# A hybrid encoder block: second chunk loaded with the first, later keys put back, merge's first attention rows in a buffer of their own, aligned tiles and equal score pieces

## The reference

```python
h = rmsnorm(x, g_norm_mix); proj = h @ w_in            # 1024 x 5168, split into the parts below
y_att = dsa_attention(q, k, v, q_idx, k_idx, w_idx)    # a relu indexer scores every visible key, the best 256 of a query are attended
y_mlstm = sigmoid(mo) * rmsnorm(mlstm_chunkwise(...))  # 4 heads of 128, causal convolution on q and k, scan over chunks
merged = sigmoid(ga) * (y_att @ w_proj_att) + sigmoid(gm) * (y_mlstm @ w_proj_mlstm)
x = x + merged @ w_out
return x + hierarchical_moe(rmsnorm(x), ...)           # 4 groups of 8 experts, top 1 group, top 2 experts
```

## Time and profile before

| | us |
|---|---|
| three runs | 3384.41, 3392.61, 3396.44 (median 3392.61) |
| the profiled execution | 3387.83, its span 3386.2 |
| TensorE busy in the span | 3001.3 (89%) |
| VectorE busy | 2481.9 (73%) |
| ScalarE busy | 1815.9 (54%) |
| TensorE's granted clock, mean | 0.949 of full speed |
| transfers | 545.93 MB, mean 161 GB/s |

### The profile page before, as it was taken

The page is one execution under the profiler, slowest core; times in us unless marked ns, Lnnn a source line. Parts: engine busy times, 40 slices in busy tenths (PEclk is TensorE's granted clock), DMA queues, the critical chain, the costliest instruction groups (busy, mean ns, idle before and its releaser), DMA issues. The chain is left out here.

```text
span 3386.2 us, 44801 instructions
## 1 busy us (share of the span) xinstructions
PE 3001.3 (89%) x12983; PEld 2228.0 (66%) x12984; DVE 2481.9 (73%) x3912; ACT 1815.9 (54%) x2527; POOL 462.2 (14%) x603
## 2 busy tenths in 40 slices
PE   7998899799899957899989689999399999999990
PEld 5766778578678724455545367787388888888870
DVE  6577599789899956766663354443799999999985
ACT  5322467577578433444434333332377777777770
POOL 0211110000000042211111000000111111111114
PEclk9999999899999979999999899999699999999995
DMA  3222533232212185536432375552578879667868
GB/s 125 88 74 70 145 119 116 77 125 86 75 60 72 66 178 123 117 90 118 91 68 65 106 214 171 164 173 93 198 267 307 333 278 364 226 254 257 309 249 340
DMA packets 382434, 545.93 MB, mean 161 GB/s; under 512 B 36624, under 2 KB 217536, under 8 KB 382160
## 3 DMA queue, kind: packets, MB, share of 16 engines
q1 hardware_dynamic: 351536, 434.81, 42.2%
q0 software_dynamic: 28448, 100.94, 7.9%
q10 hardware_dynamic: 2304, 8.39, 0.6%
HBM read 510.70 MB, written 138.19 MB: 192 GB/s over the span
## 5 line engine op out<-in xcount | busy, mean ns | idle before, releaser
L916 DVE TENSOR_TENSOR e_w_lo<-e_raw,e_w_hi 128x1024 fp32r<-128x1024 f32 x386 | 447.0, 1221 | 4.3 <-ACT e_w_hi L773 4.3
L1585 PE MATMUL x_ps<-h_hi,w_hi 128*128 128x512 f32 (+1 forms) x992 | 391.8, 395 | 6.0 <-PEq L90 4.5
L1585 PE MATMUL x_ps<-h_lo,w_hi 128*128 128x512 f32 (+1 forms) x992 | 390.1, 393 | 0.0
L1585 PE MATMUL x_ps<-h_hi,w_lo 128*128 128x512 f32 (+1 forms) x992 | 389.6, 393 | 0.0
L773 ACT CAST e_w_hi<-e_raw 128x1024 fp32r<-128x1024 f32 x386 | 377.5, 1055 | 5.7 <-PE e_pG L711 5.7
L2362 DVE CUSTOM_DVE_ANT_0 t_junk<-t_L,t_mask 128x512 bf16<-128x512 f32 (+3 forms) x320 | 186.0, 608 | 180.8 <-PE t_L L2142 179.5
L1772 DVE TENSOR_SCALAR_CACHE_REDUCE x_relu<-x_score,x_cand 128x1024 uint8<-128x1024 f32 (+3 forms) x217 | 315.7, 1487 | 3.6
L1687 ACT ACTIVATE x_relu<-x_score,x_cand 128x896 int8<-128x896 f32 (+3 forms) x217 | 281.5, 1298 | 61.9 <-DVE x_cand L1779 61.6
L2181 PE MATMUL t_O<-t_probT,t_v 128*65 128x512 f32 x544 | 288.8, 613 | 21.7 <-ACT t_probT L2334 18.7
L2334 ACT ACTIVATE t_probT<-t_ST 128x512 f32<-128x512 f32 x272 | 160.4, 594 | 271.2 <-PE t_ST L2173 270.7
L711 PE MATMUL e_pG<-e_w_hi,e_x_hi 128*128 128x512 f32 x768 | 246.8, 403 | 3.6 <-DVE e_x_lo L911 2.4
(11 more groups left out here) (415 smaller groups left out, 6266.7 us busy)
## 6 DMA issues: line engine op xcount, KB each, us to landing
e_raw<-in_w_exp_gate SPq DMA_DIRECT2D x392, 256.0 KB
e_raw<-in_w_exp_up SPq DMA_DIRECT2D x392, 256.0 KB
e_raw<-in_w_exp_down SPq DMA_DIRECT2D x192, 512.0 KB
projT<-x_out SPq DMA_DIRECT2D x120, 256.0 KB, 2.8
slot_out<-e_y POOLq DMA_DIRECT2D x48, 512.0 KB
w_raw<-in_w_in SPq DMA_DIRECT2D x40, 512.0 KB
o_gate<-projT SPq DMA_DIRECT2D x32, 512.0 KB
slot_out<-x_zeros SPq DMA_DIRECT2D x31, 512.0 KB
```

The source lines that it names most:

```text
L916: nc.vector.tensor_tensor(w_lo[:, u, :], raw[:, u, :], w_hi[:, u, :].bitcast(F32), ALU.subtract).then_inc(gl, 1)
L1585: last = nc.tensor.matmul(ps[0:w, u % 4, :], wt[:, m % 2, kk, 0:w], ht[:, kk, q * 512:(q + 1) * 512], start=(kk == 0 and s == 0), stop=(kk ...
```

## The change

- `pieces(n)` cuts a block of more than 1024 keys in equal pieces of whole 128-key blocks. The count of pieces stays. The planner's total changes with the count of 512-column matmuls.
- In the attention stage the queries of block 0 are issued by ScalarE and no longer first on SP. Quarters 2 and 3 of the keys are loaded at f = 28 and 60 and no longer at f = 3 and 7. Chunk 1 is loaded right behind chunk 0 at f = 23 and no longer at f = 34.
- In the merge the attention rows of group 0 have a buffer of their own, `Y0`, which lies over `XN` (`XN` is first written after them), and are issued before gate 0, weights 1 and gate 1, with no wait.
- Tiles are declared in another order, and 480 bytes are put behind the router's bias, so that the large tiles of the last three stages start at multiples of 512 bytes.

```diff
 def merge_and_output(pg, LG, BI):
...
-        SUM, YR, REC = sb("sums", [P, 32]), sb("y", [P, 4, W]), sb("inverse", [P, 4, W])
+        YR, REC = sb("y", [P, 4, W]), sb("inverse", [P, 4, W])
...
+        Y0 = XN[:, :, :].rearrange("p a (b n) -> p (a b) n", n=W)
...
-                    if x >= 4:
+                    if x >= 4 and g:
                         sp.wait_ge(yl, 8 * g + x - 3)
...
-                    sp.dma_start(YR[:, k % 4, :], src[:, k % 4, g * W:(g + 1) * W]).then_inc(y_in[k], 16)
+                    sp.dma_start((YR if g or k >= 4 else Y0)[:, k % 4, :], src[:, k % 4, g * W:(g + 1) * W]).then_inc(y_in[k], 16)
...
             proj_weights(0)
             rows(0, ORDER[:4])
             inverses(0)
+            rows(0, ORDER, 4)
             gates(0)
             proj_weights(1)
             gates(1)
-            rows(0, ORDER, 4)
...
-                    v.tensor_tensor(REC[:, k, :], REC[:, k, :], YR[:, k, :], ALU.mult).then_inc(n_ok, 1)
+                    v.tensor_tensor(REC[:, k, :], REC[:, k, :], (YR if g else Y0)[:, k, :], ALU.mult).then_inc(n_ok, 1)
...
 def pieces(n):
-    return [(a, min(width(n), a + 1024)) for a in range(0, width(n), 1024)]
+    step = P * -(-(n + 1) // -(-width(n) // 1024))
+    return [(a, min(width(n), a + step)) for a in range(0, width(n), step)]
...
 def attend_and_recur(pg):
...
-            load(0)
             load_keys(0)
             load(1)
...
-                if f in (3, 7):
-                    load_keys(2 + f // 7)
+                if f in (28, 60):
+                    load_keys(2 + f // 60)
...
                 k = chunk_at(f, -13)
-                if k:
+                if k and k > 1:
                     load_chunk(k)
                 if f == CHUNK0 - 9:
                     load_chunk(0)
+                    load_chunk(1)
...
+            for k in range(2):
+                act.dma_start(Q[k * AD:(k + 1) * AD, 0, :, :].bitcast(F32), queries(0)[0]).then_inc(q_in[0], 16)
+            act.dma_start(Q2[0:AD, 0, :, :].bitcast(F32), queries(0)[1]).then_inc(q_in[0], 16)
...
 def build(nc, ins, out):
...
+        c.enter_context(nc.sbuf_tensor("to_512_bytes", [P, 120], F32))
```

More of the change, by code:

```diff
@@ L144, in merge_and_output @@
         X, XN, XT, SQ = sb("x", [P, 2, DM]), sb("xn", [P, 2, DM]), sb("xT", [P, KT, P]), sb("sq", [P, DM], BF16)
-        G, WR = sb("gain", [P, DM]), sb("wr", [P, KT, NR])
+        Y0 = XN[:, :, :].rearrange("p a (b n) -> p (a b) n", n=W)
+        G, WR, SUM = sb("gain", [P, DM]), sb("wr", [P, KT, NR]), sb("sums", [P, 32])
         ss, rt, rs = (sb(n, [P, 2]) for n in ("ss", "rt", "rs"))
@@ L499, in route_and_experts @@
         w_hi, w_lo = sb("w_hi", [P, NU, 1024], F32R), sb("w_lo", [P, NU, 1024], F32R)
-        IX, IXF = sb("ix", [P, NBLK + 2], I32), sb("ix_f", [P, NBLK])
-        XG, ix = sb("xg", [P, 2, DM]), sb("ix_now", [P, 2], I32)
+        XG, Y, work = sb("xg", [P, 2, DM]), sb("y", [P, DM]), sb("work", [P, XBUF, DM])
+        IX, IXF, ix = sb("ix", [P, NBLK + 2], I32), sb("ix_f", [P, NBLK]), sb("ix_now", [P, 2], I32)
         x_hi, x_lo = sb("x_hi", [P, KT, P], F32R), sb("x_lo", [P, KT, P], F32R)
@@ L1865, in attend_and_recur @@
         sem = pg.semaphores(c, "t_")
+        idb, mxp = sb("ident_b", [P, P], BF16), sb("max_part", [P, 2, R4, 4])
         KS, K2 = sb("k", [P, AKV, SEQ], F32R), sb("k_shift", [P, AKV, SEQ], F32R)
-        V = sb("v", [P, NT, AKV, AD + 1])
         Q, Q2 = sb("q", [P, 4, AH, P], F32R), sb("q_shift", [P, 4, AH, P], F32R)
         MB = sb("mask", [P, 4, SEQ], BF16)
+        X, MN, WI = sb("m_X", [P, 2, 4, MH, P]), sb("m_MN", [P, 2, MH, P]), sb("m_WI", [P, 2, MH, P])
+        CY, YM, GN = sb("v_Y", [P, 3, 512]), sb("m_Y", [P, 2, MH, P]), sb("m_gain", [P, MH, MD])
+        OU, DEC = sb("out", [AD + 1, 3, R4, P]), sb("m_DEC", [P, MH, NT])
+        V = sb("v", [P, NT, AKV, AD + 1])
         D, ROW = sb("diag_max", [P, RING, R4, P], F32R), sb("to_row", [P, P], F32R)
-        idf, idb = sb("ident", [P, P]), sb("ident_b", [P, P], BF16)
+        idf = sb("ident", [P, P])
         junk = sb("junk", [P, 3, 512], BF16)
-        mxp, nmx = sb("max_part", [P, 2, R4, 4]), sb("neg_max", [P, RING, R4])
-        PT, OU = sb("probT", [P, 3, 512]), sb("out", [AD + 1, 3, R4, P])
+        nmx = sb("neg_max", [P, RING, R4])
+        PT = sb("probT", [P, 3, 512])
         L = c.enter_context(nc.psum_tensor("t_L", [P, 3, 512], F32))
@@ L1887, in attend_and_recur @@
         COL = sb("g_cols", [P, 4, MH, NT])
-        U, CY, TH = sb("v_U", [P, 3, HALO + 512]), sb("v_Y", [P, 3, 512]), sb("v_T", [P, 2, 512])
+        U, TH = sb("v_U", [P, 3, HALO + 512]), sb("v_T", [P, 2, 512])
         wt, bt = sb("v_w", [P, CONV, 2 * MH]), sb("v_b", [P, 2 * MH])
-        X, MN, WI = sb("m_X", [P, 2, 4, MH, P]), sb("m_MN", [P, 2, MH, P]), sb("m_WI", [P, 2, MH, P])
-        DEC, CAUS = sb("m_DEC", [P, MH, NT]), sb("m_caus", [P, P])
+        CAUS = sb("m_caus", [P, P])
         QW, AR, MP, KW, T1, T2, SQ = (sb("m_" + n, [P, MH, P]) for n in ("QW", "AR", "PT", "KW", "T1", "T2", "SQ"))
         VO, CN, N1 = (sb("m_" + n, [P, MH, E1]) for n in ("VO", "CN", "N1"))
-        GN, YM = sb("m_gain", [P, MH, MD]), sb("m_Y", [P, 2, MH, P])
         den, rec, ss, ms, rs, nw, sc = (sb("m_" + n, [P, MH]) for n in ("den", "rec", "ss", "ms", "rs", "nw", "sc"))
         magic = sb("m_magic", [P, MH], I32)
+        SUM = sb("sums", [P, NGRP - 1, 32])
         hv = lambda z: z.rearrange("p (a b) n -> p a b n", b=2)
@@ L1920, in attend_and_recur, with queries @@
         block = c.enter_context(nc.Block())
+        def queries(n):
+            return pg.d["q_parts"].rearrange("s (h d) n -> s d h n", d=AD)[:, :, :, n * P:(n + 1) * P]
         def mask_loads(n):
@@ L1930, in load @@
             def load(n):
-                src = pg.d["q_parts"].rearrange("s (h d) n -> s d h n", d=AD)[:, :, :, n * P:(n + 1) * P]
+                src = queries(n)
                 for k in range(2):
```

3 lines of the change are left out of this document (removed).

## The result

The changed kernel takes 3363.31 us (median of 5 runs, 3361.72 to 3367.65), the kernel before, on the same chip, 3390.68 (5 runs, 3381.43 to 3396.44). The ratio is 0.9927, its 95% interval 0.9916 to 0.9938: 27 us less where 26.5 were forecast, and 3363 where 3364 was. Inside, two terms were wrong in opposite directions.

The account below looks back on a forecast made before the run. TensorE and VectorE were both taken as nearly full in projection-and-index, TensorE in the experts, transfers in combining. Terms 17 + 1 + 4.5 + 0 + 4 + 0 = 26.5 us gave 3364 us, range 3354 to 3376 (3350 to 3380 holds 8 in 10).

Parts of the forecast that it names:

- Equal pieces: Score phases, blocks 8 to 13: a shorter relu-and-add loop saves 17 us in sum (9 to 21).
- the planner: Projection-and-index stage: the planner counts 24 extra score matmuls, so 1.8 us of projection work come back at the end.
- rival B: Score phases: TensorE takes over as the bound, pieces give only 8 us, total 17.5, 3374 us; chance 0.15.
- Later keys put back: Attention's carry chain: moving key quarters 2 and 3 removes TensorE's 6.63 us stall, saving 4.5 us (0 to 6.6).
- First queries on ScalarE: Attention's start: SP's 2 us of query issue ahead of the keys goes away, saving 1 us (0 to 2).
- Second chunk with the first: Attention, f = 23: nothing to win, chunk 0's stall stays; 0 us (from -6 to +1).
- Rival C: Attention: the chunk pair jams SP's queue, quarter 2 or block 8's queries come 10 us late; total 16, 3375; chance 0.06.
- Merge's first rows: Merge's start: attention rows issued earlier cut TensorE's 9.85 us wait to 5 to 6, saving 4 us (2 to 6.9).
- Aligned tiles: Merge and experts: big tiles starting on multiples of 512 bytes gain 0 us (0 to 4.6).
- rival D: Combining and starts of attention and merge: unaligned transfers take 6% longer, so alignment pays; total 33, 3358; chance 0.08.
- rival E: Experts' weight split: equal tile offsets slow VectorE's two-operand instructions; at 15% slower 3410 us; chance 0.03.
- Rival F: Score phases: something else sets the 2.44 us period, so equal pieces don't shorten it; total 9.5, 3380; chance 0.08.

Follow-up runs that it names:

- equal_old_count: Kernel before with equal score pieces, the planner charging score matmuls as with 1024-wide pieces: 3374.04 us, 0.9954 of the kernel before.
- copies kernels: Changed kernel, chunk 1 at f = 34 again, MN and WI rows laid out chunk by chunk in one or eight copies: 3342.95 and 3346.30 us.
- keys_only: Kernel before with only key quarters 2 and 3 moved to f = 28 and 60: 3380.98 us, 0.9973 of the kernel before.
- queries_sp: Changed kernel with block 0's queries issued by SP ahead of the keys again: 3364.63 us, 0.9926 of the kernel before.
- rows_act: Changed kernel, chunk 1 at f = 34 again, chunk 0's two broadcasts issued by ScalarE at f = 21: 3366.04 us, 0.9928 of the kernel before.
- rows_early: Changed kernel, chunk 1 at f = 34 again, chunk 0's two broadcasts issued by SP at f = 20: 3366.08 us, 0.9930 of the kernel before.
- plain rows: Changed kernel, chunk 1 at f = 34 again, chunk 0's MN and WI loaded from distinct projection rows, not broadcast: 3335.33 us, 0.9845.
- rows_only: Kernel before with only the merge's first attention rows in their own buffer, issued earlier: 3385.64 us, 0.9993 of the kernel before.
- equal_only: Kernel before with the equal score pieces and nothing else: 3379.84 us, 0.9969 of the kernel before.

## Why the prediction was right, and where its steps were not

**Equal pieces: right mechanism, 17 forecast, 12.7 measured** (A to D sum to 552.6 in three kernels without them, 539.9 on the mean of nine with them, equal_old_count left out). VectorE's timeline in the score phase after:

```profile
620.23 0.95 DVE L1736 TENSOR_SCALAR x_score<-x_relu,x_iw 128x640 f32<-128x640 f32 x2 [1.91 <-ACT x_relu L1664]
...
636.32 1.01 DVE L1736 TENSOR_SCALAR x_score<-x_relu,x_iw 128x640 f32<-128x640 f32 x2
...
658.61 10.44 DVE L1739 SCALAR_TENSOR_TENSOR x_score<-x_relu,x_iw,x_score 128x640 f32<-128x640 f32 x11 [0.64 <-ACT x_relu L1664]
...
672.36 5.87 DVE L1739 SCALAR_TENSOR_TENSOR x_score<-x_relu,x_iw,x_score 128x768 f32<-128x768 f32 x6 [0.41 <-ACT x_relu L1664]
...
889.18 1.22 DVE L1713 TENSOR_TENSOR w_lo<-w_raw,w_hi 128x1024 fp32r<-128x1024 f32 x1
890.31 7.74 DVE L1739 SCALAR_TENSOR_TENSOR x_score<-x_relu,x_iw,x_score 128x896 f32<-128x896 f32 x7
```

Block 8's first head starts at 620.23 and block 9's at 636.32: 16.09 us, 19.90 before. Eleven additions of block 10 (10.44 us), six of block 11 (5.87) and seven of block 13 (7.74) stand in rows that the view doesn't break. By the start times of the traces a head takes 1.71 to 1.72 us in blocks 8 and 9, 1.96 in 10 and 11 and 2.20 in 12 and 13 wherever nothing disturbs it: the forecast periods hold, and the rhythm of 2.44 us is gone from these blocks. In blocks 10 to 13 VectorE's own pair takes nearly as long (5.87 us for three in block 11), so there the loop and VectorE can't be told apart. The prediction called itself wrong if the period stayed above 2 us in blocks 8 and 9. From the first addition of a head to that of the next it is 1.94 us on the mean in block 8 (2.18, 2.06, 1.89, 1.72, 2.10, 1.71) and 2.05 in block 9 (1.71, 2.55, 1.72, 1.88, 1.72, 2.73, the last with a weight split in it). The loop is as fast as forecast, but seven of these twelve turns are disturbed, which the term had not in it.

What the term had too small is the rest. A block has only 7 steps from one head to the next, so 20.3 us and not 23.2 can be saved; for that 1.5 was taken off where it is 2.9. Then each block starts anew: relu waits for the first head's multiplication, and a block's first additions come with gaps of 0.4 to 0.8 us. ScalarE's lines by form from 620 to 690 show these waits and those for `z`:

```profile
L1664 ACT ACTIVATE x_relu<-x_z 128x640 f32<-128x640 f32 x32 | 22.3, 705 | 8.2 <-DVE x_score L1739 3.7 <-PE x_z L1605 2.4 <-DVE x_score L1736 1.6
L1664 ACT ACTIVATE x_relu<-x_z 128x768 f32<-128x768 f32 x24 | 19.3, 813 | 7.6 <-DVE x_score L1739 3.5 <-DVE x_score L1736 3.1 <-PE x_z L1605 0.5
L1664 ACT ACTIVATE x_relu<-x_z 128x512 f32<-128x512 f32 x8 | 4.8, 600 | 2.3 <-DVE x_score L1739 1.5 <-PE x_z L1605 0.8
```

The waits for the multiplication (1.6 + 3.1) and for `z` (2.4 + 0.5 + 0.8) are of one size. I had allowed 1 us for late `z` and nothing for the restarts; in this trace blocks 8 to 13 together lose 2.9 us more than what was allowed (20.3 less 1.5 for the splits and 1 for `z`, against 13.3 in A and 1.6 in blocks 12 and 13). And the planner: 1.8 forecast, 2.8 measured (B and D, 384.1 against 381.3). equal_old_count shows that no count helps: what B and D win, A loses. That fits rival B, by which TensorE has no room in the score phases, though it idles 9 of 70 us there (620 to 690); if it is B, it took a part of the gain, not most of it. No run takes the 24 matmuls away, so this isn't shown. The weight splits, last, cost no more than the 1.5 us taken: a head with one takes 1.0 and 1.1 us longer now (blocks 9 and 13), and took 0.5 and 0.7 longer before.

**Later keys put back: right mechanism, 4.5 forecast, some 5 to 8 measured.** F is 37.0 us on the mean of nine kernels with the late keys and 45.0 in four without, G 1.3 shorter (the two copies kernels left out there, whose stores lie in it), H 3.1 longer (left out there too): 6.2 in all, and keys_only by itself 6 to 12. The line that answers to TensorE's in the earlier trace rows, in the changed kernel, has no wait at all:

```profile
1242.71 0.40 PE L2175 MATMUL t_ST<-t_q,t_k 128*128 128x512 f32 x1
```

The bound was "TensorE can use at most 6.6", its idle time, and that step failed. The windows of the kernel before around the stall, which the prediction did not look at (their last three columns: granted clock, DMA share, GB/s):

```profile
1240.00:1255.00 15.00, 13.01 (x45) 6.33 (x43) 12.40 (x43) 6.06 (x11) 5.70 (x9) 1.00 0.84 179
...
1262.00:1266.00 4.00, 4.00 (x10) 1.93 (x9) 2.90 (x7) 2.58 (x5) 0.00 (x0) 0.52 0.62 161
1266.00:1274.00 8.00, 6.90 (x25) 3.31 (x23) 7.79 (x28) 3.65 (x10) 0.77 (x1) 1.00 0.76 193
```

The granted clock is 1.00 before the stall, 0.52 (the lower level, 1.2 GHz) in the 4 us behind it and 1.00 again later. The matmuls there take 0.80 and 1.91 us where the same ones take 0.40 and 1.02. A stall of this length is dearer than its idle time, here by 1.5 us. The Trainium skill, page "TensorE: Matmul & The Clock Gate", section "HAM oscillation — how this bites in real kernels", describes this case: a wait for a transfer lowers the clock, so the work behind it starts slow. The trace agrees, with 0.52. Against the gain stands H, 24.1 us on the mean of seven with the late keys and 20.9 in the four without (though 23.1 before). That quarter 2, which now goes out near chunk 0, does this is likely and not shown.

**First queries on ScalarE: 1 forecast, 0 measured, or 1 lost.** Attention's first matmul after:

```profile
1195.54 0.90 PE L2146 MATMUL t_L<-t_k,t_q 128*128 128x128 f32 x3 [22.12 <-DMA t_q_shift<-q_parts]
```

It waits as long as in the earlier trace rows and now for the queries. The 2 us of issue are saved, but the last load of the queries takes 10.1 us to land where it took 5.2 ahead of the keys in queries_sp. The prediction sized the issue and not this. The page that it named in the Trainium skill puts the gain nearer 0, and the trace agrees; rows_act fits it too, where SP's transfers came late with the broadcasts in ScalarE's queue.

**Second chunk with the first: 0 forecast, 0 to 2 lost.** SP's queue after:

```profile
1276.59 0.92 SPq L1962 DMA_DIRECT2D t_m_X<-qkT  x2
1277.55 1.06 SPq L1964 DMA_DIRECT2D t_m_X<-projT  x2
1278.65 0.51 SPq L1966 DMA_DIRECT2D t_m_MN<-m_neg_rows  x1
1279.20 0.54 SPq L1966 DMA_DIRECT2D t_m_WI<-inter_rows  x1
1279.85 3.84 SPq L1962 DMA_DIRECT2D t_m_X<-qkT  x2
1283.73 9.85 SPq L1964 DMA_DIRECT2D t_m_X<-projT  x2
1293.62 2.99 SPq L1966 DMA_DIRECT2D t_m_MN<-m_neg_rows  x1
1296.65 0.69 SPq L1966 DMA_DIRECT2D t_m_WI<-inter_rows  x1
```

The twelve issues take 20.8 us. The loads of chunk 1 fill the queue behind chunk 0's broadcasts and SP stands (9.85 us for two of them). VectorE's wait and TensorE's:

```profile
1296.57 2.14 DVE L2438 SCALAR_TENSOR_TENSOR t_m_AR<-t_m_MN,t_g_cols,t_m_caus 128x128 f32<-128x128 f32 x4 [11.42 <-DMA t_m_WI<-inter_rows]
```

```profile
1300.43 0.80 PE L2175 MATMUL t_ST<-t_q,t_k 128*128 128x512 f32 x1 [14.57 <-ACT t_probT L2342]
```

They are 11.42 and 14.57 us, before 10.55 and 13.71: the stall stayed, as forecast. Rival C's jam came, as the 20.8 us show, but not its price: quarter 2 was issued at 1306.81, 25 us ahead of the output store of f = 43 (1332.03), and from 1300 to 1345 no engine waits for a transfer.

**Merge's first rows: 4 forecast, some 4.5 measured.** TensorE's idle time in front of `o_pm`:

```profile
1910.98 0.80 PE L436 MATMUL o_pm<-o_y_hi,o_p_hi 128*128 128x512 f32 x1 [1.41 <-DVE o_y_lo L355]
...
1919.24 0.79 PE L436 MATMUL o_pm<-o_y_hi,o_p_hi 128*128 128x512 f32 x1 [4.41 <-DVE o_y_lo L355]
...
1948.11 0.80 PE L436 MATMUL o_pm<-o_y_hi,o_p_hi 128*128 128x512 f32 x1 [6.20 <-DVE o_p_lo L340]
```

The waits for `o_y_lo` are 1.41 and 4.41, together 5.8, where it was 9.85 and 5 to 6 were forecast. The 6.20 for the weights further on was 6.16 before: next to nothing was given back.

**Aligned tiles: 0 forecast, 0 to 3 measured, open.** Both tiles of this view now start on a multiple of 512 bytes:

```profile
e_work<-x SPq DMA_DIRECT2D x8, 512.0 KB, 7.8
e_raw<-x SPq DMA_DIRECT2D x8, 512.0 KB, 8.4
```

The gap of the earlier trace rows is still there (7.8 and 8.4 us), so it never was the offset, and the combining gained nothing: rival D's mechanism and place are out, and with them its 33 us. The Trainium skill's rule on pieces that the prediction weighed beside it (page "DMA: Bandwidth & Descriptors", section "How a descriptor splits into AXI transactions") is shown by no run here at 4 KB a row; whether the 3 us of L come from it is open. VectorE's multiply-add takes 1.287 us and not 1.285, and in the experts it is busy 810.93 us and not 810.68: rival E is out as well. Rival F is out by A.

The sum came out within 1 us because some 4 us too much for the pieces, 1 or 2 for the queries and up to 2 for the chunk stand against too little for the keys and perhaps the tiles. The terms as measured add up to anything from 19 to 28 us, and the two traces lie 20.3 apart, so the agreement within 1 us is luck. That the measured terms add up to a gain within the stated 15 to 36 us isn't.

## What to carry to other kernels

A loop's period after a change is the longest of several, so work out each engine's own period at the new sizes before taking the one that bound it before. A long wait of TensorE for a transfer can cost its idle time and slow matmuls behind it; read the granted clock of the microseconds after it. And where a small table is sent to all partitions again and again, lay it out so that each partition reads one long stretch: here it was worth more than any single edit of the change.

## What the chip showed that I had not expected

Two broadcasts of 256 KB, in 512-byte packets that each read one of the same four rows, held the sixteen DMA engines at 47 GB/s for 16 us, with a busy share of 0.15 (1264 to 1280 of rows_early), and transfers issued later by the same engine or another landed or issued late all the same (two loads of queries 15.4 and 17.0 us after issue in rows_act). Relaid to 2 KB packets, MN lands in 4.7 to 5.8 us (9.8 to 13.3 in the changed kernel) and WI in 4.5 to 6.9 (13.7 to 17.5). The Trainium skill, page "Perfetto Trace Analysis", section "DMA Optimizations", says that transfers under 2 KB carry an overhead each and should be made larger. These transfers are of 256 KB and only their packets are small. If the rule is read for packets, the repeated rows agree with it, but the plain rows of the same packet size, which landed in 4.8 and 5.6 us, don't show it.

Attention whose code none of them changes takes 694.9 to 701.4 us in four profiled executions, before, rows_only, equal_only and equal_old_count (first matmul to last mask matmul). A change of under 5 us there can't be read from two profiles; one has to look at the place where it acts.
